# Hyena transforms in a 256-frequency block by the symmetry of k and 255-k: even and odd times apart

## What is computed

```python
def fft_long_conv(u, k_spec, skip):
    L = u.shape[1]                                   # 256
    uf = u.astype(jnp.float32)
    y = jnp.fft.irfft(jnp.fft.rfft(uf, n=2 * L, axis=1) * k_spec[None], n=2 * L, axis=1)[:, :L]
    return (y + uf * skip.astype(jnp.float32)).astype(u.dtype)

def hyena(z, conv_w, conv_b, w1, b1, w2, b2, freq, w3, skip):
    z = short_conv(z, conv_w, conv_b)
    v, x1, x2 = jnp.split(z, HY_ORDER + 1, axis=-1)
    filt = hyena_filters(z.shape[1], w1, b1, w2, b2, freq, w3)
    y = v
    for n, gate in enumerate((x1, x2)):
        k_spec = two_sided_spectrum(filt[:, 0, n], filt[:, 1, n])
        y = gate * fft_long_conv(y, k_spec, skip[n])
    return y
```

## Time and profile before

| what | us |
|---|---|
| median of 3 executions | 2664.54 |
| lowest, highest | 2662.75, 2668.41 |
| span of the profiled execution, first to last instruction | 2672.6 |
| busy in the profiled execution: PE | 2551.9 |
| busy: DVE | 1997.6 |
| busy: ACT | 1395.7 |
| Hyena stage, first transpose to last gate | 269 to 461 |

### The profile page before, as it was taken

How to read it: one execution, slowest core, us unless ns; L and a number is a source line. 1 busy time by engine, 2 the same in 40 slices (tenths; PEclk the granted TensorE clock), 3 DMA queues, 4 the chain that set the end, 5 groups by cost and what they waited for, 6 DMA issues and landing times.

```text
span 2672.6 us, 42756 instructions
## 1 busy us (share of the span) xinstructions
PE 2551.9 (95%) x16588; PEld 2319.3 (87%) x16588; DVE 1997.6 (75%) x2574; ACT 1395.7 (52%) x2181; POOL 819.6 (31%) x765
## 2 busy tenths in 40 slices
PE   6799999999999999999999989999899999999979
PEld 3678888889977888888888879999789999999978
DVE  7889878878878785555554679898668888888855
ACT  0344334444455454445544477676556666676652
POOL 0100001002245420001111338984105555666630
PEclk8799999999999999999999989999899999999989
DMA  9988766887866885555555534444445444444434
GB/s 348 353 285 272 250 221 206 272 278 256 291 207 208 273 272 202 190 178 190 189 188 185 190 100 158 154 147 158 141 159 181 142 149 147 156 151 150 153 102 148
DMA packets 147009, 534.60 MB, mean 200 GB/s; under 512 B 16855, under 2 KB 17016, under 8 KB 146424
## 3 DMA queue, kind: packets, MB, share of 16 engines
q1 hardware_dynamic: 143480, 519.82, 58.1%
q0 software_dynamic: 3328, 12.06, 1.4%
HBM read 525.52 MB, written 6.29 MB: 199 GB/s over the span
## 4 chain that ended last, share of the span: by engine, by line
PE 71%; DVE 13%; issue 7%; ACT 6%; DMA 2%; POOL 1%; SPq 0%; ACTq 0%; DVEq 0%; POOLq 0%
PE ps L595 34%; PE ps L599 22%; PE ps L597 5%; PE ps L598 5%; DVE wl L1045 4%; ACT wh L1775 2%; DVE ps L1524 2%; DVE misc L1066 1%; DMA AF<-in_w_ada 1%; PE ps L982 1%; PE ps L728 1%; PE ps L740 1%; DVE BF L1674 1%; PE ps L657 1%; DVE BF L1664 1%
## 5 line engine op out<-in xcount | busy, mean ns | idle before, releaser
L1045 DVE TENSOR_TENSOR wl<-ring,wh 128x1024 fp32r<-128x1024 f32 x784 | 1040.8, 1339 | 392.2 <-ACT wh L1775 351.9
L599 PE MATMUL ps<-A,wl 128*128 128x256 f32 x4480 | 1265.9, 283 | 0.0
L1775 ACT CAST wh<-ring 128x1024 fp32r<-128x1024 f32 x784 | 814.6, 1044 | 356.2 <-PE ps L599 340.2
L599 PEld LDWEIGHTS ps<-A,wl 128*128 128x128 f32 x4480 | 858.0, 192 | 0.4
L595 PE MATMUL ps<-A,wh 128*128 128x512 f32 x2176 | 780.3, 403 | 24.3 <-DVE wl L1045 9.5
L597 PE MATMUL ps<-A,wh 128*128 128x256 f32 x2304 | 674.7, 293 | 15.3 <-DVE A L1049 9.8
L595 PE MATMUL ps<-B,wh 128*128 128x512 f32 x1792 | 641.4, 402 | 20.7 <-DVE wl L1045 8.7
L598 PE MATMUL ps<-A,wh 128*128 128x256 f32 x2304 | 653.9, 284 | 0.0
L595 PEld LDWEIGHTS ps<-A,wh 128*128 128x128 f32 x2176 | 412.5, 190 | 126.8 <-DVE wl L1045 10.9
L599 PE MATMUL ps<-B,wl 128*128 128x256 f32 x1792 | 504.4, 281 | 0.0
L597 PEld LDWEIGHTS ps<-A,wh 128*128 128x128 f32 x2304 | 443.7, 193 | 18.9 <-issue 10.0
(11 more groups left out here) (251 smaller groups left out, 2174.1 us busy)
## 6 DMA issues: line engine op xcount, KB each, us to landing
ring<-in_w_m SPq DMA_DIRECT2D x256, 512.0 KB, 4.6
ring<-in_hgrn_w_in SPq DMA_DIRECT2D x160, 512.0 KB, 3.8
ring<-in_w_ada SPq DMA_DIRECT2D x146, 512.0 KB, 5.2
ring<-in_w_in SPq DMA_DIRECT2D x144, 512.0 KB, 5.6
ring<-in_conv_w_in SPq DMA_DIRECT2D x96, 512.0 KB, 3.9
AF<-in_w_ada SPq DMA_DIRECT2D x46, 512.0 KB, 8.5
ring<-in_w_ab SPq DMA_DIRECT2D x32, 512.0 KB, 5.6
ring<-in_w_o SPq DMA_DIRECT2D x32, 512.0 KB, 5.6
```

Of the source, the lines that this page charges most:

```text
L599: return e.matmul(dst[:, 0:256], lo, x[:, 0, :], start=False, stop=last)
L1045: e.tensor_tensor(low[:], ring[SLOT[h]][:], hi[:].bitcast(F32), ALU.subtract).then_inc(s.lo, 1)
L1775: e.copy(wh[h % NSPLIT][:], ring[SLOT[h]][:]).then_inc(s.hi, 1)
```

## The change

The frequencies are ordered so that row j holds k = j and its partner 255-j, and times are split into even and odd. For an even time the cosine of the partner is equal and the sine negated; for an odd time the other way. So the forward transform is made for 128 frequencies only, once over the even times and once over the odd ones, without accumulation over the two (4 matmuls of 256 columns instead of 8); sum and difference of the two give the frequencies k and 255-k. ACT copies the odd part from `ps[6]` to SBUF (`yr`), because it is then read beside `ps[5]`. DVE makes sum and difference (z_low, z_high), does the complex product in six operations, and makes sum and difference again for the inverse (10 operations of 128x512 instead of 6). The inverse has 8 matmuls of 128 columns instead of 256, and gives even and odd times in separate halves of `ps[7]`, which the skip operation reads interleaved. The constant matrices are 6 tiles instead of 8. The transposes read every second time of `zh`.

```diff
-    dft = np.concatenate([tile(cos), tile(sin), tile(cos.T / 256.0), tile(sin.T / 256.0)], axis=1)
+    inverse = lambda m: (m[:, :P].T / 256.0).astype(f)[:, None, :]
+    dft = np.concatenate([tile(cos), tile(sin), inverse(cos), inverse(sin)], axis=1)
...
-        e.dma_start(dft[:, 4:8, :], d["k_dft"][:, 4:8, :]).then_inc(s.ident, 16)
+        e.dma_start(dft[:, 4:6, :], d["k_dft"][:, 4:6, :]).then_inc(s.ident, 16)
...
@@ tensor_program, hyena
-                        done = e.transpose(ps[4][:, a:a + P], zh(2 * q + c)[:, tt * P:tt * P + P], ident[:])
+                        done = e.transpose(ps[4][:, a:a + P], by_parity(zh(2 * q + c))[:, tt, :], ident[:])
...
-                for ri in range(2):
-                    w.wait_ge(s.hv, 6 * (m - 1) + 4 + ri)
-                    for mm in range(2):
-                        for tt in range(2):
-                            done = e.matmul(ps[5 + ri][:, mm * 256:mm * 256 + 256],
-                                            dft[:, 2 * ri + tt, mm * P:mm * P + P], ut[:, tt, :],
-                                            start=tt == 0, stop=tt == 1)
-                    done.then_inc(s.fwd, 1)
+                w.wait_ge(s.hv, HV * (m - 1) + 2)
+                w.wait_ge(s.odd, m)
+                for tt in range(2):
+                    for ri in range(2):
+                        done = e.matmul(ps[5 + tt][:, ri * 256:ri * 256 + 256], dft[:, 2 * ri + tt, 0:P], ut[:, tt, :],
+                                        start=True, stop=True)
+                done.then_inc(s.fwd, 1)
                 yield
-                w.wait_ge(s.hv, 6 * m + 6)
+                w.wait_ge(s.hv, HV * m + HV)
                 w.wait_ge(s.skip, 2 * m)
                 for ch in range(2):
-                    n = 0
-                    for mm in range(2):
-                        for y, base in ((yr, 4), (yi, 6)):
-                            a = mm * 256 + ch * P
-                            done = e.matmul(ps[7][:, ch * 256:ch * 256 + 256], y[:, a:a + P], dft[:, base + mm, :],
-                                            start=n == 0, stop=n == 3)
-                            n += 1
+                    for tt, z in enumerate((z_low, z_high)):
+                        for ri in range(2):
+                            a = ri * 256 + ch * P
+                            done = e.matmul(ps[7][:, ch * 256 + tt * P:ch * 256 + tt * P + P], z[:, a:a + P],
+                                            dft[:, 4 + ri, tt * P:tt * P + P], start=ri == 0, stop=ri == 1)
...
@@ vector_program, hyena
-                w.wait_ge(s.fwd, 2 * m + 1)
+                w.wait_ge(s.fwd, m + 1)
                 w.wait_ge(s.khat, 16 * m + 16)
                 w.wait_ge(s.inv, m)
-                hv.up(e.tensor_tensor(yr, ps[5][:], kr, ALU.mult))
-                w.wait_ge(s.fwd, 2 * m + 2)
-                hv.up(e.tensor_tensor(t1b, ps[6][:], ki, ALU.mult))
+                w.wait_ge(s.odd, m + 1)
+                hv.up(e.tensor_tensor(z_low, ps[5][:], yr, ALU.add))
+                hv.up(e.tensor_tensor(z_high, ps[5][:], yr, ALU.subtract))
                 w.wait_ge(s.hv, hv.n)
-                hv.up(e.tensor_tensor(yr, yr, t1b, ALU.subtract))
+                hv.up(e.tensor_tensor(two(yr), real, kr, ALU.mult))
+                hv.up(e.tensor_tensor(two(yi), imag, ki, ALU.mult))
                 w.wait_ge(s.hv, hv.n)
-                hv.up(e.tensor_tensor(yi, ps[5][:], ki, ALU.mult))
-                hv.up(e.tensor_tensor(t1b, ps[6][:], kr, ALU.mult))
+                hv.up(e.tensor_tensor(yr, yr, yi, ALU.subtract))
                 w.wait_ge(s.hv, hv.n)
-                hv.up(e.tensor_tensor(yi, yi, t1b, ALU.add))
+                hv.up(e.tensor_tensor(two(yi), real, ki, ALU.mult))
+                hv.up(e.tensor_tensor(imag, imag, kr, ALU.mult))
+                w.wait_ge(s.hv, hv.n)
+                hv.up(e.tensor_tensor(two(yi), two(yi), imag, ALU.add))
+                w.wait_ge(s.hv, hv.n)
+                hv.up(e.tensor_tensor(two(z_low), low, high, ALU.add))
+                hv.up(e.tensor_tensor(two(z_high), low, high, ALU.subtract))
...
-                    e.scalar_tensor_tensor(tmpA[ch][:], zh(i), col("hy_skip", 8 * o + i),
-                                           ps[7][:, ch * 256:ch * 256 + 256], ALU.mult, ALU.add).then_inc(s.skip, 1)
+                    back = ps[7][:, ch * 256:ch * 256 + 256].rearrange("p (a j) -> p j a", a=2)
+                    natural = lambda x: x.rearrange("p (j a) -> p j a", a=2)
+                    e.scalar_tensor_tensor(natural(tmpA[ch][:]), natural(zh(i)), col("hy_skip", 8 * o + i), back,
+                                           ALU.mult, ALU.add).then_inc(s.skip, 1)
...
@@ scalar_program, hyena
                 e.copy(ut.rearrange("p a c -> p (a c)"), ps[4][:]).then_inc(s.ut, 1)
                 yield
+                w.wait_ge(s.fwd, m + 1)
+                w.wait_ge(s.hv, HV * m)
+                e.copy(yr, ps[6][:]).then_inc(s.odd, 1)
                 yield
...
@@ gpsimd_program, spectrum
-            w.wait_ge(s.hv, 6 * m - 1)
+            w.wait_ge(s.hv, HV * (m - 1) + 7)
```

More of the change, by code:

```diff
@@ L59, in shape_constants @@
     window = np.exp((-t * deltas).astype(f)).astype(f)
-    tt = np.arange(L)[:, None]
-    kk = np.arange(L)[None, :]
+    order = np.concatenate([np.arange(0, L, 2), np.arange(1, L, 2)])
+    tt = order[:, None]
+    kk = np.concatenate([np.arange(P), 255 - np.arange(P)])[None, :]
     ang = 2.0 * math.pi * (((2 * kk + 1) * tt) % 1024) / 1024.0
     cos = np.cos(ang)
-    sin = np.sin(ang)
+    sin = np.sin(ang) * np.where(np.arange(L) < P, 1.0, -1.0)[None, :]
     tile = lambda m: np.ascontiguousarray(m.reshape(2, P, -1).transpose(1, 0, 2)).astype(f)
-    dft = np.concatenate([tile(cos), tile(sin), tile(cos.T / 256.0), tile(sin.T / 256.0)], axis=1)
+    inverse = lambda m: (m[:, :P].T / 256.0).astype(f)[:, None, :]
+    dft = np.concatenate([tile(cos), tile(sin), inverse(cos), inverse(sin)], axis=1)
     s = np.arange(P)[:, None]
@@ L73, in shape_constants @@
     masks = np.stack(masks, axis=1).astype(f)
-    return {"k_feats": np.ascontiguousarray(feats.T), "k_window": tile(window), "k_dft": np.ascontiguousarray(dft),
+    return {"k_feats": np.ascontiguousarray(feats[order].T), "k_window": tile(window[order]), "k_dft": np.ascontiguousarray(dft),
             "k_masks": np.ascontiguousarray(masks), "k_ident": np.eye(P, dtype=f)}
@@ L177 @@
 LAG = 4
+HV = 10
 SCORES = [(hd, step - 1 - LAG) for tick in HEAD_PLAN for hd, step in tick if 0 <= step - 1 - LAG < 9]
@@ L212 @@
     "hmade_v hmade_a ev pre zin zh uv gate "
-    "tr ut fwd hv inv skip y "
+    "tr ut fwd odd hv inv skip y "
     "vsum vmean vmu vsub vsq vss vn vt vtc vmx vad ug "
@@ L336, in _build @@
     ha, hn, h1, h2, h2_diff = (small[:, 512 + 256 * i:768 + 256 * i] for i in range(5))
-    dft = misc[:, 0:2048].rearrange("p (a k) -> p a k", a=8)
+    dft = misc[:, 0:1536].rearrange("p (a k) -> p a k", a=6)
     ksb = [BFf[:, 1024 * m:1024 * m + 1024] for m in range(4)]
@@ L351, in _build @@
     yi = misc[:, 3624:4136]
-    t1b = misc[:, 4136:4648]
+    z_low = misc[:, 1536:2048]
+    z_high = misc[:, 4136:4648]
     khat = XR[:, 0:4, :].rearrange("p a b -> p (a b)")
@@ L407, in head_tiles @@
         return q, kk, V, A, E, Kp, Qp
+    by_parity = lambda x: x.rearrange("p (j a) -> p a j", a=2)
     def strided(tile, offset, *dims):
@@ L825, in last_sums @@
             w.wait_ge(s.sub, 8 * norm + 4)
-            w.wait_ge(s.hv, 48)
+            w.wait_ge(s.hv, 8 * HV)
             e.matmul(mean_ap, ones[:, 2, :], sum_c, start=True, stop=False)
@@ L1216, in hyena @@
         def hyena():
-            kr, ki = khat[:, 0:512], khat[:, 512:1024]
+            two = lambda x: x.rearrange("p (m c) -> p m c", m=2)
+            kr, ki = two(khat[:, 0:512]), two(khat[:, 512:1024])
+            real = strided(misc, 1536, (4136 - 1536, 2), (1, 256))
+            imag = strided(misc, 1536 + 256, (4136 - 1536, 2), (1, 256))
+            low = strided(misc, 3112, (512, 2), (1, 256))
+            high = strided(misc, 3112 + 256, (512, 2), (1, 256))
             for m in range(8):
@@ L1851, in hyena @@
                 w.wait_ge(s.tr, m + 1)
-                w.wait_ge(s.fwd, 2 * m)
+                w.wait_ge(s.fwd, m)
                 e.copy(ut.rearrange("p a c -> p (a c)"), ps[4][:]).then_inc(s.ut, 1)
                 yield
+                w.wait_ge(s.fwd, m + 1)
+                w.wait_ge(s.hv, HV * m)
+                e.copy(yr, ps[6][:]).then_inc(s.odd, 1)
                 yield
```

## The result

Median of 20 executions 2670.27 us (2664.43 to 2675.11), of the kernel before 2667.38 (20 executions, 2662.58 to 2672.28). The ratio is 1.0013 [1.0007, 1.0019]: **slower by 0.13%**, some 3 us, where 2.0 us less was forecast. It is within the 0.2% that the prediction called no difference, and inside its range, but the interval lies on the other side of 1 than the forecast. The work on PE fell as worked out; what took its place was larger.

The account below looks back on a forecast made before the run. PE was taken to bound the Hyena stage. 10.8 us saved, less 1.4, 1.2 and 0.1, plus 0.6, gave 8.7; less clock 5.0 and 1.7, 2.0 saved: 2664.5 to 2662.5, said as 2662, range 2653 to 2671.

Parts of the forecast that it names:

- PE's work removed: Forward and inverse transforms of the Hyena stage: 3.40 us less a round, 27.2 us in 8 rounds.
- The transposes: PE's transposes reading every second element: 0 us taken, bounds 0 and a doubling, 0.43 us a round.
- The wait for the product: PE ahead of the inverse, waiting for DVE's ten operations: about 2.05 us a round, leaving 10.8 us saved.
- Rounds 1 and 7: Rounds in which DVE is late for the product: 1.4 us lost in round 1, 1.2 in round 7.
- The restart of PE: First weight load of the inverse, which can't run ahead of the product: 0.2 us, counted inside the wait.
- The clock: PE's clock halved after waits in the stage: 5.0 us for two long waits, 1.7 for one short.
- The strided read of PSUM: DVE's skip operations reading PSUM in steps of 128 elements: 0 taken, bounds 0 or 0.95 us a round.
- The start: Loading ahead of the stage, inverse constants 256 KB less: 0.6 us saved, between 0 and 0.7.
- The sum for the stage: First forward transform to the column sum after the last inverse: 193.5 us, 1.4 shorter than before.
- that of the clock falling behind nearly every wait: Rival: in the stage, six more falls at 1.7 us make it slower, 2671.0 us; chance 0.15.
- The rival of DVE as the bound: Rival: in the stage, each round as long as DVE's work, 8.1 us lost, 2670 us; chance 0.06.
- PE waiting for `wl`: Sign in the profile after: PE waiting for `wl` in this stage would mean that DVE is the bound.

Follow-up runs that it names:

- the first profile: The changed kernel's first profiled execution, nothing further edited: stage 199.94 us, PE's waits 23.9 us, four clock falls.
- the second: The changed kernel profiled once more, unedited: stage 200.62 us, PE's waits 20.5 us, six clock falls, 2674.73 us.
- the run with early chunks: The changed kernel with the double modulation chunks at blocks 18 to 20 instead of 24 to 26: stage 198.67 us, 2669.0 us.
- POOL's sums later: The changed kernel with POOL's additions waiting for the tenth product operation of DVE, not the seventh: stage 196.32 us, 2667.82 us.
- odd half first: The changed kernel with the forward transform's odd half first and signalled by itself: stage 193.25 us, 2659.49 us.
- two edits more: The changed kernel with the inverse one half later, the forward transform's odd half first and double chunks at blocks 18 to 20: ratio 0.9939 to before.

## Why the prediction was wrong

- **PE's work removed**: 27.2 predicted, 27.1 measured. Right, with 128-column records at 0.111 us as the earlier trace rows had them. The transposes cost 0.03 us more each round; I took 0.
- **The wait for the product**: 2.05 predicted, 1.98 measured where nothing disturbs it. The working (1.73 of PE, copy, ten operations at 0.69 with 0.61 or 0.73 between starts) holds step by step.
- **Beside POOL**: not in the sum, 3.25 us in rounds 3 to 6. This is the step that failed first. The prediction took DVE's durations from round 0, where POOL does nothing, and gave them to all rounds; the last two operations of ten, 0.69 us there, took up to 1.44 and 1.21. By itself this turns the 2.0 us saved into 1.3 lost.
- **Rounds 1 and 7**: 1.4 and 1.2 us beyond the common wait predicted; 3.7 and 1.1 in the first profile, 1.7 and none in the second. In that second one the clock had fallen behind rounds 5 and 6, which makes PE later and so the wait shorter; in the run with early chunks the clock fell behind both too and PE waited 1.74, and in the three in which it fell behind round 5 alone or behind neither (changed, POOL's sums later, odd half first) PE waited 3.07 to 3.33. No experiment holds the clock there. The mechanism was right; in the first profile the size of round 1 was 2.3 short.
- **The restart of PE**: 0.27 us for each wait beyond the idle time that the trace shows, 2.2 us; I had put 0.2 of it into the wait, where it did not show.
- **The clock**: 6.7 predicted, 6.0 and 10.1 left over in two profiles (the stage less work, waits and restarts). The price of a fall was right (1.6 for 1.7). The count was low in the second; in part, as I argue from the table of waits, because POOL's additions had turned waits of 2 us, of which a third cost clock, into waits of 2.4 to 2.8, of which nearly all did.
- **The strided read of PSUM**: 474 ns beside the 477 of the earlier trace rows. The bound of 0 was right. The rule of the Trainium skill that the prediction weighed ("SBUF — State Buffer", section Door 1) speaks of matmuls; on VectorE this row shows no such cost.
- **The start**: 0.6 us, not visible.

The sum for the stage: 193.5 predicted, plus 4.8 us of waits (3.25 for POOL, 2.3 in round 1, -0.7 for the rest), plus 2.2 for the restarts, less 0.7 of clock, plus 0.1, gives 199.9. Of the rivals, that of the clock falling behind nearly every wait came nearest in mechanism, and in the second profile it is what happened (six of eight). That its 2671.0 stands beside the median of 2670.27 is luck: it was 6.5 us above a median of 2664.5 from three executions, while over 20 the kernel before has 2667.38 and the change costs 2.9; and the slower time needed the microseconds of POOL, which no rival had. The rival of DVE as the bound gave 2670, but its sign, PE waiting for `wl`, is in neither profile of the changed kernel.

## What to carry to other kernels

When a change makes an operation longer or moves a release, look at what stands behind that release in the queue of every other engine, and what it will then run beside: GpSimd's additions cost nothing beside an operation with slack and their full length on the path. Work taken from the bounding engine inside a fixed interleaving also takes cover from whatever it waited for; move the consumer by as much as was removed, and here 0.13% slower became 0.4% faster by that alone, and 0.6% with two edits more. Here a wait of two microseconds for TensorE's stationary operand cost more than its length, 0.27 us for the restart each time and 1.6 us of clock in a third of the cases.

## What was not expected of the hardware

- A VectorE operation of 128x512 with both inputs in SBUF takes 1.39 us instead of 0.69 beside a GpSimd addition of 0.74 us; where the addition came 0.17 us behind the start of a VectorE operation of 1.22 us, it took 1.63 instead of 0.74 and VectorE's time stayed. In round 6 both were longer, 1.21 and 1.22 us.
- Behind one and the same wait (1.98 us, 3.25 us) the granted clock fell to 0.50 (1.2 GHz) in one execution and stayed at 1.00 (2.4 GHz) in another. Each fall lasted 3.4 us, behind the waits of 5.68, 3.68 and 4.18 us 6.8.
- 13.8 us of useless matmuls in front of the waits made the stage 6.6 us shorter in one execution, 4.5 of it by keeping the clock up.
